# Delta rule: the first two levels of the triangular inverse on 64x64 diagonal tiles

## The reference

```python
def step(state, inp):
    r_t, w_t, k_t, v_t, a_t, b_t = inp
    sa = jnp.einsum('bhij,bhj->bhi', state, a_t)
    state = (state * w_t[:, :, None, :] + sa[..., :, None] * b_t[:, :, None, :]
             + v_t[..., :, None] * k_t[:, :, None, :])
    y_t = jnp.einsum('bhij,bhj->bhi', state, r_t)
    return state, y_t
_, y = lax.scan(step, s0, xs)
```

## Time and profile before

| | |
|---|---|
| median of 3 runs | 2984.26 us (2983.17 to 2988.7) |
| the profiled execution | 2986.76 us, of which the span is 2983.7 |
| busy in the span | PE 2855.7 (96%), PEld 2602.2 (87%), DVE 2330.1 (78%), ACT 1194.1 (40%), POOL 107.3 (4%) |
| instructions | 51023 |
| mean granted PE clock | 0.984 |

### The profile page before, as it was taken

The page is one execution under the profiler, slowest core; times in us unless marked ns, Lnnn a source line. Parts: engine busy times, 40 slices in busy tenths (PEclk is TensorE's granted clock), DMA queues, the critical chain, the costliest instruction groups (busy, mean ns, idle before and its releaser), DMA issues. The chain is left out here.

```text
span 2983.7 us, 51023 instructions
## 1 busy us (share of the span) xinstructions
PE 2855.7 (96%) x19664; PEld 2602.2 (87%) x19664; DVE 2330.1 (78%) x4590; ACT 1194.1 (40%) x1720; POOL 107.3 (4%) x96
## 2 busy tenths in 40 slices
PE   6999988999999999999999999899999999999998
PEld 6998877799999998787899987778999999977886
DVE  8998665579976578888779977645898856788887
ACT  4534322234544444333355342222454444533334
POOL 0000003110000000000000000030200000000000
PEclk9999999999999999999999999999999999999999
DMA  7552431056756757888735435212567576587785
GB/s 289 189 186 106 184 127 36 8 226 203 266 193 209 277 192 265 283 288 288 244 143 185 169 111 209 69 36 92 185 225 270 177 257 229 197 298 283 281 283 195
DMA packets 208003, 593.60 MB, mean 199 GB/s; under 512 B 45968, under 2 KB 145040, under 8 KB 147216
## 3 DMA queue, kind: packets, MB, share of 16 engines
q1 hardware_dynamic: 205456, 573.53, 55.0%
q10 hardware_dynamic: 2304, 16.78, 1.3%
HBM read 537.27 MB, written 52.95 MB: 198 GB/s over the span
## 5 line engine op out<-in xcount | busy, mean ns | idle before, releaser
L1074 PE MATMUL ps<-h_hi,u_hi 128*128 128x256 f32 x2048 | 594.3, 290 | 18.3 <-DVE u_lo L1946 18.3
L1074 PE MATMUL ps<-h_lo,u_hi 128*128 128x256 f32 x2048 | 582.8, 285 | 0.0
L1074 PE MATMUL ps<-h_hi,u_lo 128*128 128x256 f32 x2048 | 582.5, 284 | 0.0
L1946 DVE TENSOR_TENSOR u_lo<-ring,u_hi 128x1024 fp32r<-128x1024 f32 x256 | 312.8, 1222 | 173.2 <-ACT u_hi L1368 172.4
L1074 PEld LDWEIGHTS ps<-h_hi,u_hi 128*128 128x128 f32 x2048 | 395.4, 193 | 21.8 <-DVE u_lo L1946 21.7
L1074 PEld LDWEIGHTS ps<-h_lo,u_hi 128*128 128x128 f32 x2048 | 395.8, 193 | 0.0
L1074 PEld LDWEIGHTS ps<-h_hi,u_lo 128*128 128x128 f32 x2048 | 395.3, 193 | 0.0
L1389 ACT ACTIVATE u_hi<-ring 128x1024 fp32r<-128x1024 f32 x192 | 203.9, 1062 | 323.7 <-PE ps L1095 323.7
L1396 ACT ACTIVATE region<-ps 128x256 f32<-128x256 f32 x256 | 98.1, 383 | 460.1 <-PE ps L1074 328.1
L1953 DVE TENSOR_TENSOR u_lo<-ring,u_hi 128x1024 fp32r<-128x1024 f32 x192 | 234.9, 1224 | 50.3 <-ACT u_hi L1389 50.0
L1368 ACT ACTIVATE u_hi<-ring 128x1024 fp32r<-128x1024 f32 x256 | 269.3, 1052 | 0.0
(11 more groups left out here) (368 smaller groups left out, 5336.0 us busy)
## 6 DMA issues: line engine op xcount, KB each, us to landing
ring<-in_stream SPq DMA_DIRECT2D x456, 1024.0 KB, 5.2
act_rows<-region SPq DMA_DIRECT2D x256, 128.0 KB, 5.3
gate_rows<-region ACTq DMA_DIRECT2D x16, 1024.0 KB, 5.8
region<-gate_rows SPq DMA_DIRECT2D x256, 64.0 KB, 3.9
region<-act_rows SPq DMA_DIRECT2D x128, 128.0 KB, 4.2
small_inverse<-act_rows SPq DMA_DIRECT2D x128, 128.0 KB, 4.2
region<-in_c SPq DMA_DIRECT2D x7, 512.0 KB, 5.6
xT<-in_x SPq DMA_DIRECT2D x1, 1024.0 KB, 10.8
```

What stands on the lines that cost most here:

```text
L1074: ins = mm(ps[:, c % 4, 0:T], x, y[:, k, :], start=k == 0 and i == 0, stop=k == KD - 1 and i == 2)
L1946: vec.tensor_tensor(u_lo[:, c % U_DEEP, :], ring[:, slot, (c % 2) * D:(c % 2 + 1) * D], u_hi[:, c % U_DEEP, :].bitcast(F32), ALU.subtract) ...
```

## The change

Levels 0 and 1 fill nothing outside the two 64x64 diagonal tiles of a matrix. The new kernel keeps only these: `XY` has 64 columns for each part, both diagonal tiles lying on top of each other in the partitions 0 to 63 and 64 to 127. Each product of levels 0 and 1 becomes two of 64x64x64, one on either half of the partitions (`corners`). The result of level 1 goes into a new full tile `Xall`, whose lower left quarter is zeroed once for each layer. Level 1 no longer forms the parts that nothing reads. Level 2 copies its corner into `Xall` instead of adding it, and the product L991 reads `Xall`. The expansions write half as much, and POOL's wait for the level 2 product of the group before instead of `u_mm`. PSUM results of a half now take one bank.

```diff
-        XY = view(18944, GRP, 2, P)
-        Z1 = view(31232, GRP, P)
+        XY, Xall = view(18944, GRP, 2, HN), view(19968, GRP, P)
+        Z1 = view(31232, GRP, HN)
...
-            where = K("block_mask").rearrange("p (z b o) -> p z b o", z=1, o=1).broadcast_to([P, 2, P // SUB, SUB])
+            where = K("block_mask").rearrange("p (z b o) -> p z b o", z=1, o=1).broadcast_to([P, 2, HN // SUB, SUB])
...
+                corners = slice(0, HN), slice(HN, P)
...
-                                q = half * 4 + s
-                                if lev < LEVELS - 1:
-                                    ins = mm(ps[:, 4 + half, s * P:(s + 1) * P], Ct[:, q, :], XY[:, q, 0, :], start=True, stop=True)
-                                else:
-                                    ins = mm(ps[HN:, 4 + half, s * HN:(s + 1) * HN], Gm[g % 2][half][0:HN, s, 0, HN:], XY[0:HN, q, 0, 0:HN],
-                                             start=True, stop=True)
+                                q, cols = half * 4 + s, slice(s * HN, (s + 1) * HN)
+                                if lev == LEVELS - 1:
+                                    ins = mm(ps[HN:, 4 + half, cols], Gm[g % 2][half][0:HN, s, 0, HN:], XY[0:HN, q, 0, :], start=True, stop=True)
+                                for rows in corners if lev < LEVELS - 1 else ():
+                                    ins = mm(ps[rows, 4 + half, cols], Ct[rows, q, rows], XY[rows, q, 0, :], start=True, stop=True)
...
-                                q = half * 4 + s
-                                if lev < LEVELS - 1:
-                                    o, c0 = half * 2 + s // 2, (s % 2) * 2 * P
-                                    mm(ps[:, o, c0:c0 + P], XY[:, q, 1, :], Z1[:, q, :], start=True, stop=True)
-                                    ins = mm(ps[:, o, c0 + P:c0 + 2 * P], Z1[:, q, :], XY[:, q, 1, :], start=True, stop=True)
-                                else:
-                                    ins = mm(ps[0:HN, half * 2, s * HN:(s + 1) * HN], Z1[HN:, q, 0:HN], XY[HN:, q, 1, HN:], start=True, stop=True)
+                                q, o = half * 4 + s, ps[:, half * 2, s * P:(s + 1) * P]
+                                if lev == LEVELS - 1:
+                                    ins = mm(ps[0:HN, half * 2, s * HN:(s + 1) * HN], Z1[HN:, q, :], Xall[HN:, q, HN:], start=True, stop=True)
+                                for rows in corners[:2 - lev]:
+                                    mm(o[rows, 0:HN], XY[rows, q, 1, :], Z1[rows, q, :], start=True, stop=True)
+                                for rows in corners if lev < LEVELS - 1 else ():
+                                    ins = mm(o[rows, HN:], Z1[rows, q, :], XY[rows, q, 1, :], start=True, stop=True)
...
-                            ins = mm(ps[:, 7, s * P:(s + 1) * P], XY[:, tt * 4 + s, 1, :], two, start=True, stop=True)
+                            ins = mm(ps[:, 7, s * P:(s + 1) * P], Xall[:, tt * 4 + s, :], two, start=True, stop=True)
...
+                            rows = slice(HN if lev == LEVELS - 1 else 0, P)
+                            A(Z1[rows, half * 4:half * 4 + 4, :], ps[rows, 4 + half, 0:4 * HN].rearrange("p (s q) -> p s q", s=4), ACT.Copy).then_inc(S["z1_copied"], 1)
...
+                vec.memset(Xall[HN:, :, 0:HN], 0.0)
...
-                            if lev < LEVELS - 1:
-                                d = ps[:, half * 2:half * 2 + 2, :].rearrange("p b (s a q) -> p (b s) a q", s=2, a=2)
+                            d = ps[:, half * 2, :].rearrange("p (s a q) -> p s a q", s=4, a=2)
+                            if lev == 0:
                                 for a in range(2):
                                     vec.tensor_tensor(XY[:, hs, a, :], XY[:, hs, a, :], d[:, :, a, :], ALU.add).then_inc(S["dxy_added"], 1)
+                            elif lev == 1:
+                                vec.tensor_tensor(XY[0:HN, hs, 0, :], XY[0:HN, hs, 0, :], d[0:HN, :, 0, :], ALU.add).then_inc(S["dxy_added"], 1)
+                                for rows in (slice(0, HN), slice(HN, P)):
+                                    ins = vec.tensor_tensor(Xall[rows, hs, rows], XY[rows, hs, 1, :], d[rows, :, 1, :], ALU.add)
+                                ins.then_inc(S["dxy_added"], 1)
                             else:
-                                corner = XY[0:HN, hs, 1, HN:]
-                                vec.tensor_tensor(corner, corner, ps[0:HN, half * 2, 0:4 * HN].rearrange("p (s q) -> p s q", s=4),
-                                                  ALU.add).then_inc(S["dxy_added"], 1)
+                                vec.tensor_copy(Xall[0:HN, hs, HN:], ps[0:HN, half * 2, 0:4 * HN].rearrange("p (s q) -> p s q", s=4)).then_inc(S["dxy_added"], 1)
...
-                    pool.wait_ge(S["u_mm"], 2 * g - 1 + half)
+                    pool.wait_ge(S["dxy_mm"], (g * LEVELS - 1) * 2 + half + 1)
```

More of the change, by code:

```diff
@@ L86 @@
 for _name, _w in (("ident", 128), ("ones", 128), ("inv_freq", 1), ("eps", 3), ("head_ones", 128), ("pair_mask", 512), ("merge_mask", 2 * 128),
-                  ("block_mask", 8), ("causal", 256), ("iota", 128), ("scan_keep", 256)):
+                  ("block_mask", 4), ("causal", 256), ("iota", 128), ("scan_keep", 256)):
     CST[_name] = (_n, _n + _w)
@@ L161, in constants @@
     put("merge_mask", np.concatenate(levels, 1))
-    put("block_mask", i // SUB == np.arange(P // SUB)[None, :])
+    put("block_mask", i % HN // SUB == np.arange(HN // SUB)[None, :])
     put("causal", np.concatenate([np.zeros((P, P)), np.where(j <= i, 0.0, -3.0e38)], 1))
@@ L440, in expansion @@
         def expansion(g, q):
-            own = Wl[:, (g % 2) * GRP + q % 2 * 4 + q // 4 * 2 + q % 4 // 2, :, :].rearrange("p a (o c) -> p a o c", o=1).broadcast_to([P, 2, P // SUB, SUB])
-            where = K("block_mask").rearrange("p (z b o) -> p z b o", z=1, o=1).broadcast_to([P, 2, P // SUB, SUB])
+            own = Wl[:, (g % 2) * GRP + q % 2 * 4 + q // 4 * 2 + q % 4 // 2, :, :].rearrange("p a (o c) -> p a o c", o=1).broadcast_to([P, 2, HN // SUB, SUB])
+            where = K("block_mask").rearrange("p (z b o) -> p z b o", z=1, o=1).broadcast_to([P, 2, HN // SUB, SUB])
             return XY[:, q, ::-1, :].rearrange("p a (b c) -> p a b c", c=SUB), own, where
```

## The result

The changed kernel takes 2968.0 us (median of 8 runs, 2960.0 to 2977.5), the kernel before beside it 2984.8 (8 runs): a ratio of 0.9942, 95% interval 0.9926 to 0.9958, some 17 us less. The forecast was 2958.4 in a range of 2950 to 2973. The sign and the range held, the size did not: two thirds of the forecast gain came.

A forecast was written before the change was run, and what follows sets the result against it. PE, busy 96%, was taken as the bound, VectorE's chain in groups 0, 2 and 3. Savings of 15.1 us a layer, 30.2, less meetings 1.0 and clock 3.3, left 25.9: 2984.3 to 2958.4 us, range 2950 to 2973.

The forecast's parts named there:

- The corners run at once: Levels 0 and 1: both 64x64 products of a pair run concurrently, 0.058 us for each pass, half of before.
- the first rival: Levels 0 and 1: corner pairs run one after the other, saving only 8 us in all, 2976 us; chance 0.13.
- Group 0: First group's levels: shorter expansions 0.9, level 0 2.4, level 1's additions 0.7; 4.0 us saved a layer, range 3.0 to 4.6.
- Group 1: Levels from second z1 half to L978, where PE's saving counts in full: 12.83 to 7.95 us, 4.9 saved.
- Groups 2 and 3: Chain up to L986, set by VectorE's order: 15.61 to 12.52 us, 3.1 saved each.
- The cap is the reciprocal: Groups 2 and 3, behind level 0: half of PE's saving is lost to VectorE's reciprocal, 3.35 us long.
- POOL meets VectorE: POOL's moved expansion can hold VectorE's substitution (group 0) and scaling (group 2): 0.25 us at each of four meetings, 1.0 in all.
- "Cost nothing" for the loads moved earlier: Loads of `Wl` for groups 2 and 3, issued earlier by SP, cost nothing: no one waits before group 1's end.
- two more falls than now (bounds 0 and 6): PE's clock in the stage: two more low stretches at 1.64 us each, 3.3 us lost.
- second rival: Delta-rule stage: small tiles with waits leave PE mostly at 1.2 GHz, 1.64 us a stretch; 2996 us at 25; chance 0.06.

The follow-up runs named there:

- the doubled products: Changed kernel with every 64x64 product of levels 0 and 1 issued twice in a row; 2982.7 us, ratio 0.9983 to the kernel before.
- wide filling: Changed kernel with unread 128x128x128 products in PE's waits, in front of groups 1 to 3 and in level 2 of groups 0, 2, 3; 2965.7 us, 0.9931.
- the late reciprocal alone: Changed kernel with VectorE's reciprocal moved behind level 1 and the scaling behind level 2, in groups 2 and 3; 2957.4 us, 0.9899.
- the same with wide filling: Changed kernel with reciprocal and scaling one level later and unread 128x128x128 products in PE's waits; 2951.9 us, 0.9884.
- the narrow to the wide filling: Narrow: changed kernel, each 128x128x128 filling product replaced by two of 64x64x64 on one tile; 2958.9 us, 0.9899; with reciprocal and scaling later 2956.1 us, 0.9894.
- the tile-by-tile order: Changed kernel with a half's products ordered by tile, all four matrices of the upper tile before the lower; 2997.9 us, 1.0037.

## Why the prediction was right or wrong

- **The corners run at once: right.** 0.68 for 16 passes, predicted 0.52 + the last pass's end. No row of before had shown two row tiles in one bank; the first rival (2976, chance 0.13), serial corners, is out. The Trainium skill's broad rule (TensorEngine Tiling (Array Packing), "Restrictions and Gotchas"), that different row tiles can't access one PSUM bank simultaneously, didn't hold here; the narrow one (PSUM — Partial Sum Buffer, "PSUM bank collisions raise a hardware error"), the same bank and the same quadrant, agrees with what ran. The first rival's own price of 8 us was not tested: the doubled products show no gain (2 us without their stalls), but the additions of their two halves at level 1 stand 1.8 us apart (493.57 and 495.37 in group 1), where the rival had 1.4.
- **Group 0: right.** From the mask to the product behind the corner 20.60 us and 16.66 after: 3.9 saved, 4.0 predicted; 5.1 in the second layer, 9.0 for both (8.0), the falls in it included. In the first layer level 0 ends 3.7 earlier (3.3 predicted), level 1's additions bring 0.4 (0.7), and the meeting with POOL costs 0.17.
- **Group 1: right but for the stall.** Undisturbed the levels take 8.30, predicted 7.95. Saved 4.5 for a layer, 9.1 for both instead of 9.8.
- **Groups 2 and 3: mechanism right, size a little off.** Where no low stretch lies in it (second layer, wide filling) the chain takes 13.19 and 12.94 us; predicted 12.52. So 2.5 each rather than 3.1, 10.2 for all four (12.4). The cap is the reciprocal, as stated: with it moved the stage is 6.6 us shorter, and undisturbed the chain takes 11.48.
- **POOL meets VectorE: right**, 0.25 in group 2 and 0.17 in group 0. That the 0.25 agrees to the digit is luck; it was picked between bounds of 0 and 1.2.
- **"Cost nothing" for the loads moved earlier: wrong**, by the stalls, 1.9 us in the profiled execution: not because anyone waited for the loads, but because PE's instructions did. No run shows that their earlier start matters for it; with them away it is gone.
- **The clock: the step that failed.** I counted "two more falls than now (bounds 0 and 6)", at 1.64. There were 44.3 us more of low clock, thirteen stretches like that of rows 2. Where I went wrong can be read in rows 8 and 9: the falls there came after waits of PE, and the change makes such waits in every group, in front of the masks and behind the last level, not only in the chains of groups 2 and 3. Those chains alone have 21.3 us more, the six stretches of the upper bound. Nothing in the rows made 6 an upper bound. The prediction's own sign of its second rival, a granted clock below 0.9 over the stage, came: it was 0.87 in either layer.

The balance: groups 1 to 3 would save 9.1 + 10.2 = 19.3 us undisturbed, the whole stage shrank by 16.4, of which group 0 is 9.0, so they saved 7.4. Of the 11.9 missing, 1.9 are stalls. The other 10, by subtraction, stand against 52.8 - 13.6 = 39.2 us more of low clock behind group 0's product that waits for the corner, 0.26 us for each. Experiments give the same size or less: from the late reciprocal alone to the same with wide filling 41.0 us of low clock go and 13.2 of stage, 2.5 of these stalls, so 0.26 each; from the narrow to the wide filling it is 24.0 and 3.9 with the late reciprocal, 0.16 each, and 20.5 and 3.8 without it and without the stalls, 0.19 each. At 0.16 the 39.2 us would make 6.3, so up to 4 us of the 10 aren't shown to be the clock's. So the second rival's mechanism was at work in part: some eleven stretches more behind that product at 0.9 each at most, not 18 at 1.64. That the price is lower because part of the low clock falls on waits for VectorE is argued; the tile-by-tile order shows what it does when it covers the levels themselves.

Against the forecast's 25.9 us the stage is 9.5 short: 6.7 by the clock (10 instead of 3.3), 1.9 by stalls, 2.2 by the chains of groups 2 and 3 and 0.7 by group 1, less 1.0 that group 0 gave more and the 1.0 set down for the meetings, which the measured chains already hold.

The Trainium skill's page TensorE: Matmul & The Clock Gate ("Part 1: The HAM clock gate") says that the clock is set by how busy PE has been recently. The trace agrees in that falls follow waits; that a busy PE is granted full speed, which one would read into it, doesn't hold in the tile-by-tile run (15.28 of 15.30 busy, 0.53 granted).

## What to carry to other kernels

Cutting TensorE's products in half on a chain of short steps turns its work into waits; count the stretches in which it will wait, in every group and in front of it too, and take at least one clock fall for each as the bad case, not a few more than now. Send neighbouring products to different tiles of the array, never one tile after the other. When a faster engine leaves another on the chain (here VectorE's reciprocal), move that step behind the faster part and fill the waits with full-size products: here the two together were worth as much again as the change itself (20 us of stage beside 16, and 0.006 of the ratio beside 0.006), and nothing without it. Where many small products run beside large loads, look at the transfers of instructions in the profile: an idle PE that no engine releases may be waiting for one.

## What the runs showed of the hardware

- Two 64x64 tiles on the diagonal of the array, writing different partitions of one PSUM bank, run at once: 0.030 us for a 64-column pass when they alternate, 0.049 when one tile's four products come before the other's.
- The granted clock was 0.53 with one tile at a time, PE busy 15.28 of 15.30 us, and 1.00 with two tiles in turn, PE busy 12.54 of 14.50.
- TensorE's instructions come in 16 KB transfers on a DMA queue, one for some 250 of its matmul and PEld instructions. Beside DMA loads of weights (DMA share 0.58 over the levels) one started 3.73 and 4.20 us behind the start of group 1's second z1 half, without them 0.96 and 1.70; with the loads TensorE stopped for 0.6 to 1.9 us, until 1.2 to 1.7 us after the transfer's end.
- VectorE's 128x512 instructions last 0.77 instead of 0.69 us beside POOL's expansion.
- Filling TensorE's waits with 128x128 products left 13.6 us of low clock in the stage, with twice as many 64x64 ones on one tile, which hold it as long, 37.6.
